# Right half of the output projection as three products of rounded parts, with the first expert weights loaded later

## What is computed

```python
merged = jax.nn.sigmoid(gate_a) * (o_a @ w_a_up[l]) + jax.nn.sigmoid(gate_b) * (o_b @ w_b_up[l])
x = x + g1 * (merged @ w_out[l])
h2 = rms_norm(x, norm2_g[l]) * (1.0 + sc2) + sh2
x = x + g2 * moe(h2, w_router[l], b_router[l], w_gu[l], b_gu[l], w_down[l], b_down[l])
```

## Time and profile before

| | |
|---|---|
| median of 3 runs | 997.53 us (996.18 to 999.67) |
| the profiled execution | 998.4 us, span of its trace 996.6 us |
| PE busy | 956.7 us of the span (96%) |
| DVE, ACT, POOL busy | 404.5, 227.2, 191.3 us |
| chain that ended last | PE 87%, DMA 5%, DVE 3%, issue 2%, ACT 1% |
| DMA | 283.96 MB, mean 285 GB/s |

### The profile page before, as it was taken

How to read it: one execution, slowest core, us unless ns; L and a number is a source line. 1 busy time by engine, 2 the same in 40 slices (tenths; PEclk the granted TensorE clock), 3 DMA queues, 4 the chain that set the end, 5 groups by cost and what they waited for, 6 DMA issues and landing times.

```text
span 996.6 us, 17022 instructions
## 1 busy us (share of the span) xinstructions
PE 956.7 (96%) x7199; PEld 517.7 (52%) x7199; DVE 404.5 (41%) x833; ACT 227.2 (23%) x488; POOL 191.3 (19%) x238
## 2 busy tenths in 40 slices
PE   3899989999999999899999999999999999999995
PEld 2676656767788746544444444443444444344442
DVE  0275967744533565323432323223232323223245
ACT  6334354443322323110010101011010101101012
POOL 2223941004200001212121111212111121211000
PEclk9999999999999999999999999999999999999998
DMA  9927623620422657989999999999999999999915
GB/s 338 341 86 253 229 84 122 242 85 16 170 85 96 242 231 262 349 301 375 377 348 372 390 387 385 389 386 397 372 397 385 388 389 379 386 370 393 381 37 182
DMA packets 71443, 283.96 MB, mean 285 GB/s; under 512 B 7488, under 2 KB 8796, under 8 KB 54984
## 3 DMA queue, kind: packets, MB, share of 16 engines
q1 hardware_dynamic: 61720, 257.93, 67.3%
q0 software_dynamic: 9648, 24.94, 9.5%
HBM read 272.62 MB, written 18.56 MB: 292 GB/s over the span
## 4 chain that ended last, share of the span: by engine, by line
PE 87%; DMA 5%; DVE 3%; issue 2%; ACT 1%; SPq 1%; POOL 0%; POOLq 0%; DVEq 0%; ACTq 0%
PE ps L1744 22%; PE ps L1480 20%; PE ps L1775 11%; PE ps L1755 11%; PE ps L1766 5%; PE ps L1692 2%; DMA ring<-in_w_ada_dram 2%; PE ps L1703 2%; PE ps L1731 2%; PE ps L1603 2%; PE ps L1532 2%; PE ps L1842 2%; PE ps L1511 1%; PE ps L1739 1%; DMA apad<-h_rows,iug 1%
## 5 line engine op out<-in xcount | busy, mean ns | idle before, releaser
L1317 DVE TENSOR_SCALAR mix<-ps 128x384 f32<-128x384 f32 x32 | 17.9, 558 | 288.3 <-ACT attn L980 288.3
L1480 PE MATMUL ps<-h_hi,wb_hl 128*128 128x512 f32 x384 | 126.0, 402 | 0.0
L700 POOL DMA_INDIRECT moe_rows<-mix,ius x31 | 47.8, 1543 | 249.4 <-DVE mix L1362 248.5
L1358 DVE SCALAR_TENSOR_TENSOR mix<-ps,WC,attn 64x512 f32<-64x512 f32 x64 | 47.9, 748 | 103.3 <-PE ps L1775 102.8
L980 ACT ACTIVATE attn<-ps 128x384 f32<-128x384 f32 x32 | 15.7, 491 | 309.1 <-PE ps L1755 309.1
L1480 PEld LDWEIGHTS ps<-h_hi,wb_hl 128*128 128x128 f32 x384 | 72.2, 188 | 19.7 <-issue 4.4
L1480 PE MATMUL ps<-h_lo,wb_hl 128*128 128x512 f32 x192 | 74.8, 389 | 0.0
L1362 DVE SCALAR_TENSOR_TENSOR mix<-ps,WC,attn 32x256 f32<-32x256 f32 x128 | 61.5, 481 | 1.9
L1744 PE MATMUL ps<-ring,mix 128*64 128x512 f32 x272 | 59.9, 592 | 0.0
L1744 PE MATMUL ps<-ring,uvp 128*64 128x512 f32 x256 | 59.0, 609 | 0.0
L619 POOL TENSOR_TENSOR wb_hl<-ring,wb_hl 128x1024 fp32r<-128x1024 f32 x16 | 38.5, 2415 | 85.1 <-ACT wb_hl L821 68.8
(11 more groups left out here) (305 smaller groups left out, 1540.6 us busy)
## 6 DMA issues: line engine op xcount, KB each, us to landing
ring<-in_w_gu_dram SPq DMA_DIRECT2D x66, 1024.0 KB, 19.0
ring<-in_w_down_dram SPq DMA_DIRECT2D x30, 1024.0 KB, 13.5
ring<-in_w_ada_dram SPq DMA_DIRECT2D x12, 2048.0 KB, 11.9
area_b<-in_w_gu_dram SPq DMA_DIRECT2D x16, 1024.0 KB, 17.9
hT<-in_w_gu_dram SPq DMA_DIRECT2D x16, 1024.0 KB, 19.6
X<-in_w_gu_dram SPq DMA_DIRECT2D x16, 1024.0 KB, 18.9
area_a<-in_w_gu_dram SPq DMA_DIRECT2D x14, 1024.0 KB, 19.3
ring<-in_w_in_dram SPq DMA_DIRECT2D x6, 2048.0 KB, 7.9
```

The costliest lines, as they stand in the source:

```text
L700: pool.indirect_dma_start(out=y_dram, in_=Y[0:slots, b, :], in_offset=None, out_offset=bass.IndirectOffsetOnAxis(ap=which, axis=0), bounds ...
L1358: v.scalar_tensor_tensor(out=Y[0:SA, b, sl], in0=ps[SA * g:SA * (g + 1), 2, :], scalar=WC[0:SA, w:w + 1], in1=g2b[0:SA, sl], op0=ALU.mult, ...
L1480: last = mm(out_, a, b, start=(n == 0 and start_), stop=(n == len(pairs) - 1))
```

## The change

The right half is now made as the left half: three products of fp32r parts per k and chunk. All rounded parts of the merged rows are therefore kept, the high ones in a new place `merged_hi` (which lies where `area_b` is) and the low ones over `mix` itself (`mix_r`). The right weights' high part goes to the ring place of `w_a_up` and the low part over the weights themselves. ACT and DVE each get eight more operations to make these parts. Since `area_b` and that ring place are in use until the projection is over, the homes are renumbered, and SP's order is: after the left half expert 0's four `w_gu` loads, after the last right chunk expert 1's four, then expert 0's `w_down`.

```diff
-        parts.enter_context(nc.sbuf_tensor("parts_gap", [P, 4096], F32))
+        merged_hi = parts.enter_context(nc.sbuf_tensor("merged_hi", [P, KD, T], F32R))
...
-        homes = [area_b[:, :], ring[slot_of[NFP - 3]], ring3[:, :], ring[slot_of[NFP - 2]], ring[slot_of[NFP - 1]],
+        homes = [ring3[:, :], ring[slot_of[NFP - 2]], area_b[:, :], ring[slot_of[NFP - 3]], ring[slot_of[NFP - 1]],
                  hT[:, :, :].rearrange("p k t -> p (k t)"), X[:, :, :].rearrange("p c d -> p (c d)"), area_a[:, :]]
...
+        right_of = [ring012_r[:, slot_of[NFP - n], :].rearrange("p (k n) -> p k n", k=KD) for n in (3, 1)]
+
         def merged_part(k, a):
-            return wb_flat[:, buffer_of(("merged", k)), a, 0:T]
+            return (merged_hi, mix_r)[a][:, k, :]
...
-            load_up(0, 0, 0)
-            load_up(0, 1, 1)
-            used(NFP - 3)
-            load_up(0, 2, 2)
-            load_up(0, 3, 3)
             sp.wait_ge(job_done, number["out", 2 * C - 2] + 1)
             for q in range(4):
+                load_up(0, q, q)
+            used(NFP - 1)
+            for q in range(4):
                 load_up(1, q, 4 + q)
-            used(NFP - 1)
             load_down(0, 0, 8)
             load_down(0, 1, 9)
...
+            front_came(act, "wo", 1)
+            act.wait_ge(u_lo_ok, 2 * KD)
+            for k in range(KD):
+                nc.scalar.activation(w_right_part(k, 0), piece("wo", 1)[:, k, :], ACT.Copy).then_inc(r_hi_ok, 1)
...
             for k in range(1, KD):
                 merged_low(k)
+            for k in range(KD):
+                dve.wait_ge(r_hi_ok, k + 1)
+                v.tensor_tensor(w_right_part(k, 1), piece("wo", 1)[:, k, :], w_right_part(k, 0),
+                                ALU.subtract).then_inc(r_lo_ok, 1)
             dve.wait_ge(rows_in, 64)
...
             for ch in range(C):
                 b_ = start("out", 2 * ch + 1)
-                w = have("wo", 1)
                 for k in range(KD):
-                    last = mm(b_, mT[:, k, ch * P:(ch + 1) * P], w[:, k, :], start=(k == 0), stop=(k == KD - 1))
+                    pe.wait_ge(r_lo_ok, k + 1)
+                    for a, b in ((0, 0), (0, 1), (1, 0)):
+                        last = mm(b_, merged_part(k, a)[:, ch * P:(ch + 1) * P], w_right_part(k, b),
+                                  start=(k == 0 and a + b == 0), stop=(k == KD - 1 and a == 1))
                 last.then_inc(job_done, 1)
```

More of the change, by code:

```diff
@@ L79, in trunk, with rounded @@
         ada_dram = nc.dram_tensor("ada_rows", (4, D), F32).ap()
+        def rounded(name, shape):
+            over = ExitStack()
+            t = over.enter_context(nc.sbuf_tensor(name, shape, F32R))
+            over.close()
+            return t
+        ring012_r = rounded("ring012_r", [P, 3, 4096])
         ring012 = sb("ring012", [P, 3, 4096])
+        mix_r = rounded("mix_r", [P, KD, T])
         mix = sb("mix", [P, 4096])
@@ L308, in trunk @@
         o_used = sem("o_used")
+        r_hi_ok, r_lo_ok = sem("r_hi_ok"), sem("r_lo_ok")
         h_hi_ok, h_lo_ok = sem("h_hi_ok"), sem("h_lo_ok")
@@ L412, in trunk, with w_right_part @@
         wb_flat = wb_hl[:, :, :, :, :].rearrange("p b a k n -> p b a (k n)")
+        right_of = [ring012_r[:, slot_of[NFP - n], :].rearrange("p (k n) -> p k n", k=KD) for n in (3, 1)]
         def merged_part(k, a):
-            return wb_flat[:, buffer_of(("merged", k)), a, 0:T]
+            return (merged_hi, mix_r)[a][:, k, :]
         def w_out_part(k, a):
-            return wb_flat[:, buffer_of(("merged", k)), a, T:T + CH]
+            return wb_flat[:, buffer_of(("merged", k)), a, 0:CH]
+        def w_right_part(k, a):
+            return right_of[a][:, k, :]
         def buffer_of(kb):
```

## The result

| | median | runs | ratio to before |
|---|---|---|---|
| before | 997.63 us (996.18 to 999.67) | 4 | |
| after | 1005.71 us (1005.2 to 1006.62) | 4 | 1.0079 (1.0062 to 1.0095) |

The change costs 8.1 us. The forecast was 999.6 with a range up to 1004.5, so the time lies outside. It comes within 0.1 us of the second rival's 1005.6, but the mechanism of that rival isn't what happened, as the experiments show. The profiled execution took 1006.62 us, its span is 1004.8 us, 8.2 longer than before.

A forecast was written before the change was run, and what follows sets the result against it. PE, busy 96% of the span, was taken as the bound, with latencies deciding from 382 to about 421 us. 998.4 - 1.5 + 2.6 + 1.0 = 1000.5, as a median 999.6 us, range 994.5 to 1004.5.

The forecast's parts named there:

- the second rival: Also the backlog rival: token-weight write and gather wait out the longer load backlog, 7 us, giving 1005.6 us; chance 0.2.
- the sum: Profiled 998.4, less 1.5 saved, plus 2.6 for the clock and 1.0 for the moved loads: 1000.5 us.
- PE's products: Right half: 24 fp32r products replace 16 fp32 instructions per chunk, 5.44 us for 6.95, 6.0 us less over four chunks.
- DVE's eight operations: Eight low parts ahead of the row operation and left halves take 4.9 us; right chunk 0 is taken 1.5 us later.
- the cover of 3.41 us: DVE's earlier wait for right chunk 0, which the 4.9 us of new DVE operations would exceed.
- TensorE's clock: After PE's 5.5 us idle before the first transposes the clock falls, mostly in chunk 2, costing 2.6 us.
- the two cases taken: Earlier clock falls in the trace, lasting 3.4 and 6.9 us at the 1.2 GHz level, used to bound the new fall.
- the saving of 1.5: Right half: of the 6.0 us PE saves on products, only 1.5 us reaches the end of the last right chunk.
- The price of 1.9: Extra time of 32 products at expert 1's rows under the lowered clock, 9.05 us against 2 x 3.60.
- The moved loads: Expert 0's and 1's later loads crowd the token-weight write and gathers on the chain: 1.0 us, bounds 0 and 11.
- No fall of the clock: First rival: PE's idle time before the first transposes brings no lower clock, 2.6 us less, 997.0 us; chance 0.2.
- The saving comes through: Third rival: DVE's new operations overlap better, right chunk 0 taken at 355.1, saving 4.5 us: 994.0 us; chance 0.08.

The follow-up runs named there:

- experiment 1: Kernel before with 64 more waiting PE instructions at PE's start, nothing of the change in it: 1005.35 us, ratio 1.0079.
- 2: Changed kernel with 128 more waiting PE instructions at PE's start: 1000.22 us, ratio 1.0025 against the kernel before.
- 5: Changed kernel with PE's count load, comparison and overflow block taken out, so no jump: 998.25 us, ratio 1.0003 against the kernel before.
- 10: Changed kernel without PE's overflow block and jump, timed again in a later batch: 999.3 us, ratio 1.0013 against the kernel before.
- experiment 6: Changed kernel with 44 filler products before the first transposes and PE's code 256 instructions longer than before ahead of the jump: 997.47 us, ratio 0.9983.
- experiment 11: Kernel before without PE's overflow block and jump, plus 24 filler products before expert 1's rows: 995.63 us, ratio 0.9982.
- experiment 3: Kernel before with only the new homes and new order of the loads, right half still fp32: 998.41 us, ratio 1.0015.
- experiment 4: Changed kernel with 128 filler instructions and ACT's and DVE's new operations spread over the left half: 995.21 us, ratio 0.9972 against the kernel before.

## Why the prediction was wrong

- **The step that failed** is the sum: "998.4 - 1.5 + 2.6 + 1.0 = 1000.5". It takes for granted that everything behind expert 31 stays as it is, because no line of it is edited. Missing is a term of +6.5 us in the span: 4.0 us more waiting behind PE's jump over the overflow block, 2.95 us at half the clock behind it, 0.4 made up. It is shown from four sides: 64 instructions alone bring the wait and the slow product (1), 128 more or no jump take them away (2, 5), and without the jump the rest of the change is 1.3 us (10), within 1 us of the forecast's net 2.1. That the wait is one for code rests on less: on the code transfer that falls into it in both kernels that have the wait, on its being "issue", and on the two transfers that the page has fewer without the jump.
- **PE's products** were right: 24 products where 16 were, two chunks done 10.9 us after the start of the right half, as 2 x 5.44 says.
- **DVE's eight operations** were right: 4.90 us for 4.9 forecast, and the cover of 3.41 us used up. PE's idle time is 5.15 us for 5.5.
- **TensorE's clock** had the right mechanism and too high a price. The fall lasts 3.4 us, the lower of the two cases taken, and costs 1.4 us (experiment 6) where the sum has 2.6. The last right chunk is done 32.8 us after the start of the right half (350.75 to 383.56), 0.1 more than before, at the lower edge of the 32.8 to 34.5 forecast. Without the fall it is 31.4 (experiment 6: 351.67 to 383.12), so the saving of 1.5 was 1.2. The price of 1.9 taken from the earlier trace rows counts the first 32 products alone; by experiment 11 that fall of 6.9 us costs 3.1, nearer to the 3.4 that the prediction gives beside it. The 2.6 was too much because this fall lasted half as long.
- **The moved loads** have the size of the 1.0 us but not its reason. In the changed kernel's chain that ended last:

```profile
402.62 5.47 DMA h_rows<-wts
```

and in PE's timeline:

```profile
421.71 1.54 PE L1753 MATMUL ps<-ident,apad 96*128 96x96 f32 x8 [2.78 <-DMA apad<-h_rows,iug]
```

The write takes 5.47 us for 5.80 before, and PE's wait grows from 1.93 to 2.78. Expert 1's gather is slower: from its issue to the transposes it is 410.56 to 421.71, 11.15 us, for 409.71 to 419.67, 9.96, before; experiments 2, 5 and 10 have 10.9 to 11.2. But with the loads alone (experiment 3) it is 410.36 to 420.48, 10.1 us, and before without the jump 10.2. So the moved loads aren't shown to be the cause, and what slows this gather in the changed kernel stays open. The gathers of the whole kernel:

```profile
DMA to landing us min/median/max: 7.2/9.6/11.1
```

against 4.5, 9.7 and 10.7 in the earlier trace rows.
- **The backlog rival** gave 1005.6, next to the time measured, for a mechanism that wanted 7 us and is worth 1.5 us by experiment 3's ratio, 2.9 at the upper end. That the number fits is luck. Without the experiments the number would have "confirmed" it.
- **No fall of the clock**, the first rival, is false for this kernel; in experiment 4, behind 2.44 us of idle time before the transposes, the clock stayed, and behind 5.15 it fell. The length alone doesn't decide it: before expert 1's rows it fell behind 1.13 us (experiment 1).
- **The saving comes through**, the third, is false too, and also only by where DVE's operations stand. Spread over the left half they bring the kernel to 995.21, 1.2 from the 994.0 given for it. "DVE's order is fixed" was true of the change and not of the idea.

What stays open: at which offsets the jump is dear. Against the kernel before, only shifts of 0, +64, +192 and +256 instructions were measured; +64 alone is dear, so how much code is loaded at a time of the jump isn't mapped. Open too is why the early fall of the clock lasts 3.2 us in some executions and 6.8 in others, what slows expert 1's gather, and what share of its 10 us is bandwidth.

## What to carry to other kernels

Any edit that adds instructions to an engine ahead of a long block that is jumped over can change the cost of that jump, by about 6.5 us here (5.5 to 7.5 by the medians of experiments 2, 5 and 10); after such an edit compare the ends of the two traces first, look for a wait that ends in "issue" right behind a branch, and shift the code by filler instructions, or leave the branch out, before the edit itself is judged. Operations added for a helper engine belong into its gaps while the loop ahead still runs, not in a row behind it: the same sixteen operations were worth 5.0 us by where they stood. An idle time of PE in front of dense work is paid twice, in waiting and in clock; filler products of its length give the second part back, also where the wait itself can't be shortened.

## What the runs showed of the hardware

- A transfer of code is 0.97 MB / 59 = 16.4 KB. Where one falls into the wait behind PE's jump, with the DMA engines 98.1% busy with data, that wait is 4.0 us longer: 4.51 and 4.52 us for 0.52, in two different kernels.
- Over the end of that wait and the 16 products behind it the clock was 0.69 for 11 us, and the products took 10.06 us for 7.11.
- Idle times of 1.13, 1.93, 2.11, 2.78, 3.24 and 5.15 us were followed by 3.2 to 6.9 us at the 1.2 GHz level, with no order by their length; one of 2.44 us by none. 3.4 us at that level cost 1.4 us in the right half, 6.9 us cost 3.1 behind expert 1's rows.
- With 4.2 MB more in SP's queue (experiment 3) the small write took 5.80 us as before and expert 1's gather 10.1 for 9.96.
